# V of a sliding-window attention, turned by VectorE in 32x32 squares and a round trip through DRAM instead of by eight TensorE transposes

## What is computed

```python
h = rms_norm(x, pre_norm)                       # (1024, 1024)
proj = h @ w_in                                 # q, k, v, gate_a, u, v_b, gate_b, mg_a, mg_b
# q: 16 heads of 64; k and v: 2 heads of 64, so v is (1024, 128)
scores = q . k over this block of 128 keys and the one before, + bias, sink
out = softmax(scores) @ v
y_a = (out * silu(gate_a)) @ w_branch_a
...
x = x + rms_norm((sigmoid(mg_a) * y_a + sigmoid(mg_b) * y_b) @ w_out, post_norm)
```

## Time and profile before

| | us |
|---|---|
| median of 3 runs | 911.77 |
| their range | 909.92 to 911.94 |
| the profiled execution, its own time | 907.86 |
| its span | 906.1 |

### The profile page before, as it was taken

How to read it: one execution, slowest core, us unless ns; L and a number is a source line. 1 busy time by engine, 2 the same in 40 slices (tenths; PEclk the granted TensorE clock), 3 DMA queues, 4 the chain that set the end, 5 groups by cost and what they waited for, 6 DMA issues and landing times.

```text
span 906.1 us, 12649 instructions
## 1 busy us (share of the span) xinstructions
PE 898.7 (99%) x4332; PEld 754.0 (83%) x4332; DVE 640.1 (71%) x1135; ACT 491.0 (54%) x948; POOL 499.4 (55%) x395
## 2 busy tenths in 40 slices
PE   9999999999999999999999999999999999999997
PEld 7888888888888888888888888888888888888886
DVE  6766794655656564656565678688689878989968
ACT  6554355766756675757566664344444434534563
POOL 4565235777686868695868685445542252043236
PEclk9999999999999999999999999999999999999999
DMA  8889764422222253323222243533188550435004
GB/s 307 195 200 247 243 204 106 136 77 90 71 91 85 82 139 129 94 77 98 72 84 91 82 150 95 187 122 122 59 303 323 186 209 1 139 116 210 1 1 186
DMA packets 126591, 122.50 MB, mean 135 GB/s; under 512 B 23208, under 2 KB 95936, under 8 KB 126272
## 3 DMA queue, kind: packets, MB, share of 16 engines
q1 hardware_dynamic: 124288, 118.27, 41.2%
q10 hardware_dynamic: 2240, 3.43, 1.2%
HBM read 89.68 MB, written 35.15 MB: 138 GB/s over the span
## 4 chain that ended last, share of the span: by engine, by line
PE 98%; ACT 0%; DVE 0%; POOL 0%; issue 0%; DVEq 0%; POOLq 0%; ACTq 0%
PE acc L970 51%; PE acc L1150 11%; PE acc L823 9%; PE ps_m L1150 7%; PE ps_t L1150 7%; PE ps_t L987 3%; PE ps_m L1017 3%; PE acc L913 2%; PE ps_t L997 2%; PE ps_t L853 1%; PE ps_m L853 0%; PE acc L1042 0%; PE ps_t L839 0%; PE ps_t L855 0%; PE ps_m L855 0%
## 5 line engine op out<-in xcount | busy, mean ns | idle before, releaser
L970 PE MATMUL acc<-mv,w_hi 128*128 128x512 f32 x1344 | 353.1, 392 | 0.0
L970 PEld LDWEIGHTS acc<-mv,w_hi 128*128 128x128 f32 x1344 | 245.0, 188 | 45.0
L970 PE MATMUL acc<-mv,w_lo 128*128 128x512 f32 x672 | 181.1, 391 | 0.0
L970 PEld LDWEIGHTS acc<-mv,w_lo 128*128 128x128 f32 x672 | 126.2, 188 | 28.3
L1751 POOL TENSOR_TENSOR w_lo<-sums,w_hi 128x1024 fp32r<-128x1024 f32 x48 | 116.0, 2418 | 46.4 <-ACT w_hi L1316 38.4
L1751 POOL TENSOR_TENSOR w_lo<-raw,w_hi 128x1024 fp32r<-128x1024 f32 (+1 forms) x48 | 95.7, 1994 | 41.5 <-ACT w_hi L1309 35.9
L1150 PE MATMUL acc<-right,left 128*128 128x512 f32 x432 | 98.7, 389 | 0.0
L1150 PEld LDWEIGHTS acc<-right,left 128*128 128x128 f32 x432 | 81.0, 188 | 17.2 <-DVE left L2131 0.4
L1796 POOL TENSOR_SCALAR_AFFINE_SELECT pt_prev<-pt_pack 128x512 fp32r<-128x512 f32 x64 | 41.7, 652 | 85.7 <-DVE pt_pack L2067 85.7
L1518 ACT ACTIVATE prob<-neg_s,neg_max 128x129 f32<-128x129 f32 x128 | 50.6, 397 | 68.6 <-DVE neg_max L2076 68.5
L823 PE MATMUL acc<-mv 128*128 128x512 f32 x288 | 69.3, 394 | 0.6 <-ACT mv L1183 0.6
(11 more groups left out here) (282 smaller groups left out, 1680.8 us busy)
## 6 DMA issues: line engine op xcount, KB each, us to landing
raw<-in_w_in SPq DMA_DIRECT2D x56, 512.0 KB, 4.0
ht_d<-sums SPq DMA_DIRECT2D x8, 512.0 KB, 5.1
mix_d<-mix_b SPq DMA_DIRECT2D x8, 512.0 KB, 3.9
ga_d<-gate SPq DMA_DIRECT2D x16, 256.0 KB, 2.0
tb<-tb_d SPq DMA_DIRECT2D x4, 1024.0 KB, 5.2
ub<-mix_d SPq DMA_DIRECT2D x7, 512.0 KB, 3.5
gb_d<-ub SPq DMA_DIRECT2D x7, 512.0 KB, 2.6
x_both<-in_x SPq DMA_DIRECT2D x6, 512.0 KB, 6.3
```

The costliest lines, as they stand in the source:

```text
L970: ins = nc.tensor.matmul(bank, (w_lo if y == 2 else w_hi)[:, left + k * P:left + (k + 1) * P], right[:, (OPW if y == 1 else 0) + k * HALF: ...
```

## The change

The eight transposes, and ScalarE's copy of `ps_m` to `gate[1]`, are taken out. VectorE, after `mix_read(NT - 1)`, turns `gate[0]` in place: every 32x32 square of it by itself. SyncE stores that tile in a new DRAM tensor, waits for it, and loads it into `gate[1]` with the squares at their places, by four DMAs of 32 partitions each. `load_pair(1, 1)` moves on SyncE from behind `load_k(0)` to before this. ScalarE's `v_hi(0)` moves to s = 2 of pair 0, ahead of `left_hi(0, 4)`, behind a wait for the four DMAs; `v_hi(1)` moves from s = 2 to s = 4. On VectorE the difference moves to s = 2, behind the same wait, `v_lo(0)` to s = 4 and `v_lo(1)` to s = 5.

```diff
@@ -157,6 +157,7 @@
     tb_d = nc.dram_tensor("tb_d", [KT, P, SEQ], f32)
     ga_d = nc.dram_tensor("ga_d", [KT, P, SEQ], f32)
     gb_d = nc.dram_tensor("gb_d", [KT, P, SEQ], f32)
+    v_turned_d = nc.dram_tensor("v_turned_d", [P, SEQ], f32)
     v_d = nc.dram_tensor("v_d", [P, 2 * NT * P], i32)
     bias_d = nc.dram_tensor("bias_d", [N_HEADS, BIAS_ROW], f32)
     skew_d = nc.dram_tensor("skew_d", [N_HEADS, P, BIAS_ROW], f32)
@@ -277,8 +278,8 @@
         raw_in = [sem(f"raw_in{i}") for i in range(3)]
         kvh_ok, kvl_ok, k_done, v_done = sem("kvh_ok"), sem("kvl_ok"), sem("k_done"), sem("v_done")
         khi_ok, klo_ok, k_out, k_in = sem("khi_ok"), sem("klo_ok"), sem("k_out"), sem("k_in")
-        vf_ok, vt_done, vs_ok, vd_ok, vhi_ok, vlo_ok, v_out, v_in = (
-            sem("vf_ok"), sem("vt_done"), sem("vs_ok"), sem("vd_ok"), sem("vhi_ok"), sem("vlo_ok"), sem("v_out"), sem("v_in"))
+        vf_ok, v_turn_ok, v_squares, vd_ok, vhi_ok, vlo_ok, v_out, v_in = (
+            sem("vf_ok"), sem("v_turn_ok"), sem("v_squares"), sem("vd_ok"), sem("vhi_ok"), sem("vlo_ok"), sem("v_out"), sem("v_in"))
         h_in = [sem(f"h_in{b}") for b in range(2)]
         t_ok, thi_ok, tlo_ok = sem("t_ok"), sem("thi_ok"), sem("tlo_ok")
 
@@ -717,11 +718,17 @@
             sp.wait_ge(klo_ok, 1)
             sp.dma_start(k_d[1, :, :], k_tmp[1][:, :].bitcast(i32)).then_inc(k_out, 16)
             spill_mix(NT - 1)
+            load_pair(1, 1)
+            sp.wait_ge(v_turn_ok, 1)
+            sp.dma_start(v_turned_d[:, :], gate[0][:, :]).then_inc(v_squares, 16)
             for b in range(2):
                 sp.wait_ge(mix_out[b], 16 * NT // 2)
+            sp.wait_ge(v_squares, 16)
+            for g in range(4):
+                sp.dma_start(gate[1][32 * g:32 * (g + 1), :].rearrange("a (t q b) -> a t q b", t=NT, q=4),
+                             v_turned_d[:, :].rearrange("(q a) (t g b) -> g a t q b", q=4, t=NT, g=4)[g]).then_inc(v_squares, 16)
             sp.wait_ge(k_out, 32)
             load_k(0)
-            load_pair(1, 1)
 
             for n in range(PAIRS):
                 for s in range(7):
@@ -1099,9 +1106,6 @@
             product(0, 1)
             product(0, 2)
             pe.wait_ge(mix_ok, NT)
-            for t in range(NT):
-                ins = nc.tensor.transpose(ps_m[:, t * P:(t + 1) * P], gate[0][:, t * P:(t + 1) * P], ident[:, :])
-            ins.then_inc(vt_done, 1)
             for s in range(1, 7):
                 product(0 if STEPS[s] != 1 else 1, STEPS[s])
             for n in range(1, PAIRS - 1):
@@ -1607,12 +1611,11 @@
             left_hi(0, 6)
             evict_1(0)
             left_hi(0, 5)
-            act.wait_ge(vt_done, 1)
-            nc.scalar.activation(gate[1][:, :], ps_m[:, :], ACT.Copy).then_inc(vs_ok, 1)
-            act.wait_ge(vs_ok, 1)
-            v_hi(0)
             for s in range(7):
                 if s == 2:
+                    act.wait_ge(v_squares, 80)
+                    v_hi(0)
+                if s == 4:
                     act.wait_ge(vd_ok, 1)
                     v_hi(1)
                 after(0, s)
@@ -2478,6 +2481,8 @@
             left_sums_2(0)
             t_lo(3)
             mix_read(NT - 1)
+            dve.wait_ge(vf_ok, 1)
+            nc.vector.transpose(gate[0][:, :], gate[0][:, :]).then_inc(v_turn_ok, 1)
 
             def v_lo(d):
                 dve.wait_ge(vhi_ok, d + 1)
@@ -2488,12 +2493,14 @@
                         view[:, d, :, 0, :].bitcast(f32), ALU.subtract)
                 ins.then_inc(vlo_ok, 1)
 
-            dve.wait_ge(vs_ok, 1)
-            own.link(nc.vector.tensor_copy(gate[0][:, 0:P], gate[1][:, 0:P]))
-            nc.vector.tensor_tensor(gate[0][:, P:SEQ], gate[1][:, 0:SEQ - P], gate[1][:, P:SEQ], ALU.subtract).then_inc(vd_ok, 1)
-            v_lo(0)
             for s in range(7):
+                if s == 2:
+                    dve.wait_ge(v_squares, 80)
+                    own.link(nc.vector.tensor_copy(gate[0][:, 0:P], gate[1][:, 0:P]))
+                    nc.vector.tensor_tensor(gate[0][:, P:SEQ], gate[1][:, 0:SEQ - P], gate[1][:, P:SEQ], ALU.subtract).then_inc(vd_ok, 1)
                 if s == 4:
+                    v_lo(0)
+                if s == 5:
                     v_lo(1)
                 after(0, s)
             for n in range(1, PAIRS):
```

## The result

| | before | changed |
|---|---|---|
| median of 10 runs, us | 909.93 | 913.71 |
| their range | 908.05 to 912.43 | 911.54 to 916.94 |
| the profiled execution, its own time | 907.86 | 913.86 |
| its span | 906.1 | 912.0 |

The ratio is 1.0042, with a 95% interval of 1.0025 to 1.0059: the kernel became slower by 0.42%, 3.8 us. Before's median of 909.93 is that of ten runs; the three runs that stood ahead of the prediction had 911.77. The profiled execution of before (907.86) was a short one of its kind, so the two spans lie 5.9 us apart.

What follows compares the result with a forecast made beforehand. TensorE was taken to bound the kernel, busy 898.7 of 906.1 us. Removing the transposes (-0.89) and a wait for V (+1.2) gave +0.3 us on the median of 911.77, so 912.1, range 909.9 to 915.0.

Steps and rivals of the forecast that it cites:

- the likeliest case: At product (0, 3): V in gate[1] at 152.8, TensorE waits 1.2 us, kernel 0.3 us slower; chance 0.50.
- rival 2: At product (0, 3): V late enough to tell, a long wait and perhaps half clock, 914.6 or 916.1 us; chance 0.15.
- The long end of V's path: Latest time T at which V stands in gate[1] after store and loads: 155.3, giving 914.6 us.
- The gain: On TensorE between products (0, 2) and (0, 6): removing the eight transposes saves 0.89 us.
- The place: TensorE would wait at product (0, 3), which adds into the bank that evict_4(0) reads, if T is over 151.6.
- Who waits for V: ScalarE at s = 2 of pair 0: evict_4(0) behind V's wait ends at T + 2.3, T being V's arrival.
- margins of the other edits: c_22, GpSimd's low part, K and bias stay hidden; c_22 and K by 1.6 us each.
- The squares: Four loads of V into gate[1] in 128-byte pieces: 6.5 us, with ends at 6.2 and 7.9.
- The store: V's squares to DRAM, issued about 141.0 behind two transfers: landing taken as 146.3, between 144.5 and 147.4.
- The clock: TensorE's clock may halve after 1.4 to 3.4 us of waiting, costing 2.7 us; forecast as staying at 1.00.
- The sum: Whole kernel: -0.89 for the transposes and +1.2 for the wait, +0.3 us.
- rival 3: V's copies in squares many times slower than plain ones: kernel 34 us slower, 946; chance 0.01.

Runs made afterwards that it cites:

- e3_no_transposes: The kernel before without its eight transposes, ScalarE copying V unturned (values not the reference's); 907.71 us, ratio 0.9978.
- e0_again: The changed kernel measured again with no edit; 913.0 against 909.09 us for before, ratio 1.0034.
- e2_wait_filled: The changed kernel plus 16 matmuls without use where TensorE waits; 911.66 us, ratio 1.0028 to before.
- e8_squares_wait_for_store_only: The changed kernel with V's store ahead of w's load and the mixing spill, the squares' loads waiting for the store alone; 910.05 us, ratio 1.0021 to before.
- e5_store_alone: The changed kernel with V's store ahead of w's load and the mixing spill, squares issued after the spill's landing; 912.93 us, ratio 1.0048 to before.
- the first experiments: The earlier of the follow-up runs, with before measured again beside each group of kernels on its chip; no single time.

## Why the prediction was right and where it was wrong

The range held the time, and the median moved up as forecast. But the likeliest case was not what happened: I gave a wait of 1.2 us and a time 0.3 us above before, and it was rival 2, with a chance of 0.15, that came, wait and clock both.

That the time lies in the range is in good part luck. The range stood on 911.77, and ten runs of before gave 909.93, 1.8 us less. As changes, the range went from 1.9 us less to 3.2 us more, and the measured change is 3.8 us more. The long end of V's path, T = 155.3, was met (155.27), but not by its own terms: the store was later than its long end and the squares quicker than theirs. And at that end the wait is 3.7 us, over the 3.4 by which the clock had fallen at the end of the span, so by the prediction's own rows the clock's 2.7 us belonged into the upper end, which would then have been 917 and more. A base too high made up for a wait and a clock that were too small. Point by point:

- **The gain**, 0.89 us: right, shown by e3_no_transposes and by the starts of the products. The 390 ns apiece that the Trainium skill lists for a 128x128 bf16 tile (VectorE: DVE Perf Modes, The three transpose paths) would have made 3.1 us of it. The starts above don't agree: eight float32 transposes in a row took 0.79 us.
- **The place**: right. What waited was product (0, 3), for `evict_4(0)`, as the step "Who waits for V" said. T + 2.3 was T + 2.4. None of the margins of the other edits gave way: no wait of TensorE names K, the bias, `c_22` or GpSimd's low part. Moving ScalarE's and VectorE's steps removed the loss but for the 0.3 us before the scores.
- **The squares**: 6.5 us taken, 6.3 measured (148.93 to 155.2), on the empty queue that the step had argued.
- **The store: the first step that failed.** I took 5.3 us from issue to landing and at most 6.4 (147.4); it was 7.9. With the squares' 0.2 us taken off, that puts T 2.4 us later, and with it the wait from 1.2 us to near 3.8. I had a lone store at 3.5 us, priced the two transfers ahead at the 364 GB/s of a stretch with long rows among them, 1.44 us each, and then took less than the sum. Measured, a lone store took 3.9 to 5.5 us, one transfer ahead made it 5.8 and two 7.5 to 8.2, so the second adds about 2 us. In the windows of after the DMA share is high but moves only 194 GB/s at 142 to 143, when the spill and the load of w, both in short rows, are under way, then 403 GB/s when the store itself flows, and after 147 a last 26 GB/s with a share of 0.07. I read that as a few DMA engines still at work when the others are through, and the store has landed only when all are; which they are, and why, was not tried, and neither was the part that the length of the rows has in it.
- **The clock: the second.** I had the mechanism and a bound from the trace, a fall after 1.4 to 3.4 us of idleness, and left it outside the range because the wait was to be 1.2 us. With 3.8 us of wait it fell, and cost 2.9 us in that execution and 1.7 in e0_again's, where I had put 2.7. e2_wait_filled takes it away alone.
- **The sum.** With the measured terms it is -0.9 + 3.8 + 2.9 = 5.8 us, the difference of the spans. The medians differ by 3.8. Before's profiled execution lies 2.1 us under its median, since a part of its executions take up to 3 us and more longer than the rest (below), while that of after lies at its median.
- **The copies in pieces of 128 bytes** (rival 3) were not many times slower, as the rows of x had said: 512 KB in 6.3 us on an empty queue, where a plain load of as much lands in 4.0. The Trainium skill's factor of 19 for strided copies (VectorE: DVE Perf Modes, The three transpose paths) is one against the DMA's own transpose, where the innermost step of the destination is large. No run here has that transpose or such a step; nothing near such a factor is seen against the plain load.

## What to carry to other kernels

A value that is replaced on a busy engine by a detour over DRAM is bought with latency, so first look for what stands behind its wait in the program of each engine: here the detour was harmless, and one eviction queued behind its wait cost six times the gain (5.3 against 0.89 us, between the medians with and without it), and with V's steps later it cost almost nothing. Price a DMA by what stands ahead of it in its queue as measured for a like pair, not by the best rate of the trace. Where TensorE bounds a kernel, price a wait with the clock as well: after the waits of 1.8 us and more that were profiled here around V, the products at half the clock cost another 1.7 to 2.9 us. And carry a forecast as a change against before, so that a base from three runs can't hide a miss.

## What the runs showed that I had not expected

The waits that left the clock full and those that made it fall lie close together: 1.5 us of wait left it full, 1.8 made it fall, with one profile of each. The clock also doesn't always fall inside the wait. In e8_squares_wait_for_store_only TensorE was at work again from 155.5 and the clock went down after that, so that product (0, 3) began at full and ended at half clock.

The profiled execution of e5_store_alone took 917.84 us, while its four others took 912.7 to 913.3. It had a second wait, in the first stage (TensorE's waits):

```profile
PE acc L977 <- ACT c L1372: 4.3, 1, 4.3
PE acc L830 <- DVE mv L1925: 2.6, 1, 2.6
```

VectorE's transpose of the last squares of x, and the windows (columns as above) after it:

```profile
94.75 1.25 DVE L1908 STREAM_TRANSPOSE sums<-x_both 128x1024 f32<-128x1024 f32 x1 [5.85 <-DMA x_both<-in_x]
```

```profile
99.00:101.40 2.40, 0.00 (x0) 0.00 (x0) 2.38 (x5) 1.85 (x3) 1.25 (x1) 1.00 0.65 199
101.40:103.00 1.60, 1.55 (x5) 1.27 (x6) 1.53 (x4) 0.00 (x0) 0.00 (x0) 0.72 0.90 289
```

The squares of x came 2.4 us later than in before's trace, TensorE waited 2.6 us, and its clock fell to half after work had been taken up again: the same chain as with V, 50 us earlier, in a part that before has as well. Before's executions spread too: of the 35 beside the first experiments most took 907.6 to 909.6 and nine 911.4 to 911.9, with a few between. That the long ones are the same event fits in size, but none of them was profiled, so it stays open.
